# Hybrid decoder step on one core: the low weight parts of the input projection move from GpSimd to VectorE

## The reference, cut to what matters

```
proj = rmsnorm(x) @ w_in                    # (520, 2048) @ (2048, 3848), the "projection"
z, xbc, dt, u5, gate_b, gate_c, hv, upool = split(proj)
mix = [ssd(xbc, dt, z) | s5(u5) | short_conv(gate_b, gate_c, hv) | pool(upool)]
h = x + rms(mix) @ w_out
h = h + cross_attention(rmsnorm(h), k, v)   # k, v = rmsnorm(mem) @ w_k, w_v for the prompt
h = h + relu(rmsnorm(h) @ w_up)^2 @ w_down
y = rmsnorm(h)
```

## Time and profile before

| | us |
|---|---|
| median of 3 timed runs | 2900.38 |
| profiled execution | 2896.25 |
| its span, first to last instruction | 2894.1 |
| TensorE busy | 2821.1 (97%) |
| VectorE busy | 877.8 (30%) |
| ScalarE busy | 775.1 (27%) |
| GpSimd busy | 1195.9 (41%) |

### The profile page before, as it was taken

How to read it: one execution, slowest core, us unless ns; L and a number is a source line. 1 busy time by engine, 2 the same in 40 slices (tenths; PEclk the granted TensorE clock), 3 DMA queues, 4 the chain that set the end, 5 groups by cost and what they waited for, 6 DMA issues and landing times.

```text
span 2894.1 us, 53723 instructions
## 1 busy us (share of the span) xinstructions
PE 2821.1 (97%) x22196; PEld 2701.3 (93%) x22196; DVE 877.8 (30%) x1311; ACT 775.1 (27%) x984; POOL 1195.9 (41%) x516
## 2 busy tenths in 40 slices
PE   7999899999999999999999999999999999999998
PEld 6999898777899988699999999999999999999998
DVE  4777645555522334422211000110001100011223
ACT  5221124424332211222323112222122221222222
POOL 2455334565443322344344444444444434444442
PEclk9999899999999999999999999999999999999999
DMA  6733344544533565533333333333333333333332
GB/s 186 139 97 97 78 128 155 156 158 156 168 90 87 181 202 193 176 94 94 91 91 94 91 90 94 88 94 93 88 94 88 94 94 87 94 90 91 94 89 94
DMA packets 505743, 329.84 MB, mean 114 GB/s; under 512 B 31013, under 2 KB 458899, under 8 KB 504207
## 3 DMA queue, kind: packets, MB, share of 16 engines
q1 hardware_dynamic: 470488, 294.02, 34.5%
q10 hardware_dynamic: 35163, 34.52, 4.1%
HBM read 309.02 MB, written 19.76 MB: 114 GB/s over the span
## 4 chain that ended last, share of the span: by engine, by line
PE 82%; DVE 6%; issue 6%; POOL 4%; ACT 1%; DMA 1%; SPq 0%; POOLq 0%; DVEq 0%; ACTq 0%
PE lin L1401 75%; POOL wlo L802 3%; POOL wlo L760 1%; PE aux L1712 1%; PE aux L1667 1%; DVE turn L1990 1%; PE lin L1607 1%; DVE y L1999 1%; DVE rot L1990 1%; PE aux L1658 1%; PE aux L1557 0%; PE aux L1553 0%; PE lin L1480 0%; DVE ca L1990 0%; DMA raw<-in_w_in 0%
## 5 line engine op out<-in xcount | busy, mean ns | idle before, releaser
L760 POOL TENSOR_TENSOR wlo<-raw,whi 128x1024 fp32r<-128x1024 f32 x428 | 1035.3, 2421 | 1535.8 <-ACT whi L839 1338.6
L839 ACT ACTIVATE whi<-raw 128x1024 fp32r<-128x1024 f32 x380 | 401.7, 1058 | 1416.6 <-PE lin L1401 1277.8
L1401 PE MATMUL lin<-fl,whi 128*128 128x260 f32 x2048 | 578.4, 282 | 0.0
L1401 PE MATMUL lin<-fh,wlo 128*128 128x260 f32 x2048 | 578.0, 282 | 0.0
L1401 PE MATMUL lin<-ml,whi 128*128 128x260 f32 x2048 | 577.6, 282 | 0.0
L1401 PE MATMUL lin<-fh,whi 128*128 128x260 f32 x2048 | 577.6, 282 | 0.0
L1401 PE MATMUL lin<-mh,whi 128*128 128x260 f32 x2048 | 577.5, 282 | 0.0
L1401 PE MATMUL lin<-mh,wlo 128*128 128x260 f32 x2048 | 577.3, 282 | 0.0
L1401 PEld LDWEIGHTS lin<-fh,wlo 128*128 128x128 f32 x2048 | 385.9, 188 | 0.0
L1401 PEld LDWEIGHTS lin<-mh,wlo 128*128 128x128 f32 x2048 | 385.6, 188 | 0.0
L1401 PEld LDWEIGHTS lin<-ml,whi 128*128 128x128 f32 x2048 | 385.5, 188 | 0.0
(11 more groups left out here) (428 smaller groups left out, 4467.2 us busy)
## 6 DMA issues: line engine op xcount, KB each, us to landing
raw<-in_w_up SPq DMA_DIRECT2D x128, 512.0 KB, 4.0
raw<-in_w_down SPq DMA_DIRECT2D x128, 512.0 KB, 3.9
raw<-in_w_in SPq DMA_DIRECT2D x60, 512.0 KB, 3.9
raw<-in_w_out SPq DMA_DIRECT2D x32, 512.0 KB, 3.9
raw<-in_w_q SPq DMA_DIRECT2D x32, 512.0 KB, 4.0
piece<-in_cache_mem_k SPq DMA_DIRECT2D x32, 512.0 KB, 6.1
piece<-in_cache_mem_v SPq DMA_DIRECT2D x32, 512.0 KB, 5.2
raw<-in_w_o SPq DMA_DIRECT2D x32, 512.0 KB, 3.9
```

The source lines that it names most:

```text
L760: pool.tensor_tensor(wlo[:, slot, :], raw[:, slot % 2, :], whi[:, slot, :].bitcast(F32), ALU.subtract).then_inc(s.w_lo, 1)
L839: act.activation(whi[:, slot, :], raw[:, slot % 2, :], ACT.Copy).then_inc(s.w_hi, 1)
L1401: mm = pe.matmul(lin[:, 2 * i + f, 0:HALF], w, m[:, k, HALF * f:HALF * f + HALF], start=(n == 0 and part == 0), stop=(n == KT - 1 and part ...
```

## The change

GpSimd no longer makes the low parts of units 8 to 51. It runs `input_weights(0)` to `(3)` one after the other, each as soon as its inputs allow, and then waits until VectorE has made 12 of the 16 low parts of the memory rows (`mem_lo`) before it starts on the low parts of the key and value weights. VectorE gets a helper `lo_weights`, which waits for the high part of unit n and makes the low part. In its loop, at the head of position n (5 to 48), it makes the low part of unit n + 3. At n = 5 it first waits for the seventh step of GpSimd's own count, the end of `input_weights(0)`, behind which GpSimd makes no low part any more until the key and value weights. This low part does not wait for its own end.

```diff
             for T in range(1, 4):
                 lo_turn(T)
             input_weights(0)
-            for n in range(8, 52):
-                lo_unit(2 + n // 4, n % 4)
-                if n - 3 in S5_A[0:3]:
-                    input_weights(S5_A.index(n - 3) + 1)
+            for f in range(1, 4):
+                input_weights(f)
+            pool.wait_ge(s.mem_lo, 12)
             with pool.Fori(T_KV, T_KV + KVX) as T:
...
+            def lo_weights(n):
+
+                v.wait_ge(s.w_hi, 8 + n + 1)
+                v.tensor_tensor(wlo[:, n % 4, :], raw[:, n % 2, :], whi[:, n % 4, :].bitcast(F32),
+                                ALU.subtract).then_inc(s.w_lo, 1)
+
...
             s5_weights(0)
             for n in range(4, 52):
+                if n == 5:
+                    v.wait_ge(s.pool_own, 7)
+                if 5 <= n < 49:
+                    lo_weights(n + 3)
                 if n == 4:
```

## The result

| | before | changed |
|---|---|---|
| median of the timed runs, us | 2900.26 | 2883.50 |
| profiled execution, us | 2896.25 | 2885.67 |
| its span, us | 2894.1 | 2883.6 |
| TensorE's mean granted clock | 0.988 | 0.990 |
| VectorE busy, us | 877.8 | 874.3 |

The medians lie 16.8 us apart. The ratio is 0.9948 with a 95% interval of 0.9932 to 0.9964, which is 15.1 us less, within 10.4 to 19.7. One of the five timed runs of the changed kernel, 6894.95 us at a mean granted clock of 0.402, is left out of the ratio; the median of the other four is 2883.34. The forecast was 2884, within 2872 to 2893.

A forecast was written before the change was run, and what follows sets the result against it. VectorE's lateness in the projection, from GpSimd's low parts stopping its instructions, was taken to cost TensorE 30.8 us. 26.7 us gained less 10.2 us for a new wait gives 16.5: 2900.38 to 2884 us, range 2872 to 2893.

The forecast's parts named there:

- Each low part on GpSimd stops the VectorE instruction that meets it: In the projection, a GpSimd low part lengthens the VectorE instruction meeting it by about 2.02 us.
- 44 low parts at 1.25 us on VectorE: Low parts of units 8 to 51 take 1.224 us each on VectorE, 1.25 with the gap between instructions.
- No wait in parts 1 and 2 and for `ca` of part 3, and no surplus: TensorE's projection waits of 1.13, 5.46 and 4.91 us vanish with their slow clock; for `ca` perhaps a few tenths stay.
- Part 0: `hc` at 178, a wait of 1.0 us, 3.11 us of slow clock, 4.1 us left: Before the products with part 0's states, 4.1 of 9.5 us remain; `hc` at 178, the middle of 174.1 and 181.5.
- `input_weights` sooner costs nothing: GpSimd's S5 weights run sooner and are needed many units later: nothing; an extra meeting in part 0 left out of the sum.
- A new wait at position 41, 8.6 + 1.6 = 10.2 us: TensorE's third pooling product waits for `pool_out(1)`, queued behind unit 44's late low part: 8.6 us plus 1.6 us slow clock.
- The other waits at the heads of positions cost nothing: VectorE's other waits for conversions are covered by a unit's slack; without cover, up to 1.25 us at each of 44 positions.
- 30.8: Cost in us of VectorE's lateness in the projection before: four TensorE waits, 15.87 us, plus 14.89 us of slow-clock surplus.
- All behind the projection only shifts: TensorE's wait at the projection's end for VectorE's last memory low parts, and everything after, only shift: no cost.
- no wait at position 41: Rival, chance 0.10: the new wait before the third pooling product does not occur; 2873.7 us, or 2870 if part 0 is free.
- VectorE the bound: Rival, chance 0.06: VectorE becomes the bound, low parts being pure load on the four chains; slower, 2925.6 us.
- The smaller gain: Rival, chance 0.16: part 0 waits as before and the clock stays low behind parts 1 and 2; 4.9 us gained, 2895.5.

The follow-up runs named there:

- e2: Changed kernel, but VectorE makes only the low parts of units 36 to 51 and GpSimd units 8 to 35 as before: 2911.0 us, ratio 1.0043.
- e4: Changed kernel plus two useless GpSimd subtractions reading SBUF per unit 8 to 51, `input_weights(1)` to `(3)` back among the units: 2915.0 us.
- e5: As e4, but the useless GpSimd instructions are fills that only write the spare tile: 2879.9 us, ratio 0.9922.
- r1: The changed kernel measured again, nothing altered: 2885.1 us, ratio 0.9945 against the kernel before.
- e1: Changed kernel with VectorE's pooling output put ahead of the low part at each position's head: 2875.2 us, ratio 0.9914.
- e3: Changed kernel, but GpSimd makes the last eight low parts, units 44 to 51: 2875.3 us, ratio 0.9913.
- e6: e1 plus GpSimd's `input_weights(1)` held back until VectorE has made the states of part 0: 2870.2 us, ratio 0.9896.

## Why the prediction was right

Point by point, by its own steps.

- *Each low part on GpSimd stops the VectorE instruction that meets it.* Right for instructions with both inputs in SBUF, for copies and for scalar forms; an instruction with an input in PSUM was not stopped (last section). In the changed kernel the `scn` copies fell from 1732 to 359 ns, and e2 brings them back; e4 against e5 shows that it takes GpSimd's reads.
- *44 low parts at 1.25 us on VectorE.* 1.277 us. The excess over the earlier trace rows is `input_weights` meeting a few of them.
- *No wait in parts 1 and 2 and for `ca` of part 3, and no surplus.* Right: none is in the trace, and the two windows are at 1.00.
- *Part 0: `hc` at 178, a wait of 1.0 us, 3.11 us of slow clock, 4.1 us left.* `hc` came at 179.55, which is 178.2 on the clock of the trace before (1.36 us earlier), and the wait was 1.41 us. The middle of the two bounds was a choice, and that it fits is partly luck; the standing at conversions that it stood for measured 3.56 us (1.68, 0.26 and 1.62). The window took 15.14 us at 0.66 against 10.51 us at 1.00, 4.63 us of slow clock: 6.0 us left. The term was too small by 1.9 us, most of it the clock. I took the surplus from the shortest wait of before, but it is not proportional to the wait: 3.11 us behind 1.13 us, 4.63 behind 1.41, 5.09 behind 4.37. In r1, e1 and e3 the same stretch behind waits of 1.6 to 1.9 us takes 15.1 to 15.3 us too.
- *`input_weights` sooner costs nothing.* Nearly right: the meeting was there before at 4.2 us and measured 4.9. Of the 0.7 us more, 0.55 are the low part of 1.78 us, the additional meeting that the prediction named and kept out of its sum. What the prediction overlooked is that the meeting could be taken away, for about 5 us of the kernel's time (e6).
- *A new wait at position 41, 8.6 + 1.6 = 10.2 us.* 8.31 us of waiting, and 8.36 us from there to the end of the next unit, where the same work without a slow clock takes 6.62 us: 1.74 us, together 10.05. e1 and e3 give 9 to 10 us back. The 6.62 us are 405.15 to 411.77 in the trace of before, at 1.00. The order was as forecast too: output, two memory loads, weights, conversion, low part, pooling output. From the output's end to the start of the pooling product it took 389.71 - 377.16 = 12.55 us, where the forecast had 413.7 - 401.2 = 12.5.
- *The other waits at the heads of positions cost nothing.* Right. VectorE stood 43.0 us for ScalarE's conversions (the row of 44 low parts) and TensorE waited for none of the low parts in the projection.

The sum: 30.8 - 6.0 - 10.05 leaves 14.7, and a wait of 0.3 us for an eviction (at 158.22 us of the trace before) has gone: 15.1 us, which is what the stage gained. The forecast of 16.5 was 1.5 us high, the term of part 0 being the cause. *All behind the projection only shifts* was wrong as well: the key and value stage gave some 2 us back, in both traces of the changed kernel. By the traces the change is therefore worth some 13 us, 3.5 below the forecast. The medians lie 16.8 us (in r1 15.7 us) apart; that they come closer to 16.5 is luck within the scatter of the runs, whose interval reaches from 10.4 to 19.7 us.

Of the rivals, "no wait at position 41" is refuted by the row of 8.31 us, and e1 is that rival made true: 2875.2 us against its 2873.7. "VectorE the bound" is refuted by the short forms and by e1 (2875.2 with all the same low parts on VectorE). The smaller gain was right in one half of one point, part 0's clock. What I would add to the rivals is e2's case: the forecast was the difference of two terms, 26.7 and 10.2 us, that have nothing to do with each other, and with the first one missing the change is slower (2911.0).

## What to carry to other kernels

When work moves into an engine's in-order queue, look first at what it waits for and what stands behind it there: 43 low parts cost TensorE nothing, and the one whose weights came late cost 10 us until the statement behind it was put first. Where GpSimd and VectorE share a stage, price a GpSimd instruction by the VectorE instructions that it meets on the way to TensorE's next wait, and look also at the meetings that a change leaves in place. And price a short wait of TensorE at its length and the slow clock behind it: here 1.4 us took 4.6 us more.

## What the runs showed of the hardware

- A GpSimd instruction that only fills SBUF (528 ns for 128x512, 88 of them in e5) did not lengthen VectorE's products with two inputs; subtractions of the same shape (1393 ns) did. Copies and one-input forms grew beside fills by up to 0.4 us (a copy of 128x23 from 0.18 to 0.58 us).
- A meeting costs up to the rest of the GpSimd instruction, whatever the size of VectorE's, where both of VectorE's inputs lie in SBUF, or it is a copy or a scalar form (0.49 us became 1.57 in e6): 0.17 us of copying became 2.25 us, and a product of 0.76 us became 1.5 to 1.6 us beside instructions of about 1.4 us. A sum with one input in PSUM (`stg`, from `lin`) kept its 0.70 us beside a GpSimd addition, at 157.47 us of the trace before.
- A wait of 1.41 us left a granted clock of 0.66 over the 15.14 us behind it, between the levels of 1.2 and 2.4 GHz. One of 8.31 us ahead of full units left 0.79 over 8.36 us. The same stretches without a wait ran at 1.00 (10.61 us in e6). The first has many small products behind the wait, the second a unit of large ones; that this makes the difference was not tried.
